# Two sums of squares: eight TensorE ones-matmuls each, or seven GpSimd adds and one ones-matmul

## The reference, cut to what matters

```python
o = jnp.einsum('bse,ed->bsd', merged, w_out[l])
x = x + g1 * rms_norm(o, g_post_mix[l])                 # "x2" in the kernel

h2 = rms_norm(x, g_pre_ffn[l]) * (1.0 + sc2) + sh2      # needs sum over d of x2 * x2
f = jnp.square(jax.nn.relu(jnp.einsum('bsd,df->bsf', h2, w_ff1[l])))
f = jnp.einsum('bsf,fd->bsd', f, w_ff2[l])
x = x + g2 * rms_norm(f, g_post_ffn[l])                 # "x3"
...
h = rmsnorm(x, norm1_g)                                 # second block; needs sum over d of x3 * x3
```

## Time and profile before

| | us |
|---|---|
| median of three runs | 2803.28 (2801.44 to 2804.9) |
| span of the profiled execution, first to last instruction | 2799.7 |
| PE busy | 2694.0 (96%) |
| DVE busy | 1879.8 (67%) |
| ACT busy | 1327.5 (47%) |
| POOL busy | 267.3 (10%) |

### The profile page before, as it was taken

The page is one execution under the profiler, slowest core; times in us unless marked ns, Lnnn a source line. Parts: engine busy times, 40 slices in busy tenths (PEclk is TensorE's granted clock), DMA queues, the critical chain, the costliest instruction groups (busy, mean ns, idle before and its releaser), DMA issues. The chain is left out here.

```text
span 2799.7 us, 41619 instructions
## 1 busy us (share of the span) xinstructions
PE 2694.0 (96%) x16618; PEld 2115.0 (76%) x16618; DVE 1879.8 (67%) x2866; ACT 1327.5 (47%) x1941; POOL 267.3 (10%) x429
## 2 busy tenths in 40 slices
PE   7999999999999999999999989888999999999998
PEld 4856644777888888877778888777778888888886
DVE  7678987567665466684987616765656576646676
ACT  4147765567555434464441114452334655543344
POOL 0115630001000000000000001110000110000000
PEclk9999999999999999999999999999999999999999
DMA  7721100446566888732464241216233666677884
GB/s 270 222 79 33 55 1 1 143 155 240 204 232 222 300 279 292 256 116 64 136 160 145 106 144 56 82 43 217 94 132 128 211 216 229 231 290 257 293 287 152
DMA packets 205906, 474.00 MB, mean 169 GB/s; under 512 B 49040, under 2 KB 69648, under 8 KB 199376
## 3 DMA queue, kind: packets, MB, share of 16 engines
q1 hardware_dynamic: 187792, 393.73, 42.5%
q0 software_dynamic: 17920, 77.61, 7.1%
HBM read 344.09 MB, written 124.29 MB: 167 GB/s over the span
## 5 line engine op out<-in xcount | busy, mean ns | idle before, releaser
L2199 PE MATMUL psum<-merged_operand 128*128 128x512 f32 x1536 | 360.8, 390 | 0.0
L2199 PEld LDWEIGHTS psum<-merged_operand 128*128 128x128 f32 x1536 | 288.5, 188 | 60.6
L2199 PE MATMUL psum<-h_half_operand 128*128 128x512 f32 x1344 | 316.8, 391 | 0.0
L2199 PEld LDWEIGHTS psum<-h_half_operand 128*128 128x128 f32 x1344 | 252.4, 188 | 55.3 <-issue 1.0
L2199 PE MATMUL psum<-h_half_operand,weight_parts_operand 128*128 128x512 f32 x768 | 177.5, 392 | 0.8 <-DVE weight_parts_operand L2706 0.6
L2199 PEld LDWEIGHTS psum<-h_half_operand,weight_parts_operand 128*128 128x128 f32 x768 | 143.6, 188 | 34.0 <-DVE weight_parts_operand L2706 2.7
L3694 PE MATMUL psum<-x_operand,weight_high 128*128 128x512 f32 x448 | 140.9, 396 | 2.1 <-DVE z_mixed L3311 2.1
L3694 PE MATMUL psum<-o_operand,weight_high 128*128 128x512 f32 x448 | 138.5, 390 | 0.0
L3694 PE MATMUL psum<-x_operand,weight_low 128*128 128x512 f32 x448 | 138.1, 389 | 0.0
L2706 DVE TENSOR_TENSOR weight_parts_operand<-weight_ring,weight_parts_operand 128x1024 fp32r<-128x1024 f32 x66 | 80.7, 1223 | 84.1 <-ACT weight_parts_operand L2356 83.8
L2706 DVE TENSOR_TENSOR h_half_operand<-o,h_half_operand 128x1024 fp32r<-128x1024 f32 (+1 forms) x58 | 74.1, 1298 | 71.7 <-ACT h_half_operand L2491 51.0
(11 more groups left out here) (657 smaller groups left out, 5941.5 us busy)
## 6 DMA issues: line engine op xcount, KB each, us to landing
o<-in_w_ff SPq DMA_DIRECT2D x80, 512.0 KB, 4.7
merged<-hidden_terms SPq DMA_DIRECT2D x56, 512.0 KB, 5.8
hidden_upper<-in_w_ff_down SPq DMA_DIRECT2D x48, 512.0 KB, 4.8
weight_ring<-in_w_out SPq DMA_DIRECT2D x32, 512.0 KB, 3.4
hidden_terms<-weight_parts POOLq DMA_DIRECT2D x16, 1024.0 KB
hidden_terms<-weight_ring POOLq DMA_DIRECT2D x16, 1024.0 KB, 8.2
hidden_upper<-in_w_ff_up SPq DMA_DIRECT2D x32, 512.0 KB, 4.6
o<-hidden_terms SPq DMA_DIRECT2D x28, 512.0 KB, 5.9
```

Of the source, the lines that this page charges most:

```text
L2199: mm = pe.matmul(bank, w[:, at:at + P], tiles(r, i), start=opens and m == 0, stop=closes and m == 2, skip_group_check=resumed)
```

## The change

The two groups X2_0 and X3_1 get the taker POOL. GpSimd adds the eight squares of a group in place into the first, seven 128x512 adds in a chain; each waits for its square and for the add before it. PE then sums the joined tile alone: for X2_0 in the middle of mixing step 13, for X3_1 ahead of the sums of `acc_early` and Y_0L. ACT waits for one count in place of eight.

```diff
-        SQUARES = [("PE", KT), ("DVE", KT), ("DVE", OUTS), ("DVE", OUTS), ("DVE", OUTS), ("PE", KT), ("DVE", OUTS - 1), ("PE", 1),
-                   ("PE", KT)]
+        SQUARES = [("POOL", KT), ("DVE", KT), ("DVE", OUTS), ("DVE", OUTS), ("DVE", OUTS), ("POOL", KT), ("DVE", OUTS - 1),
+                   ("PE", 1), ("PE", KT)]
...
-                def sum_first_x(many):
-                    for t in many:
-                        wait(pe, sq_made, begin[X2_0] + t + 1)
-                        sum_of(0, tiles(o, t), begins=t == 0, ends=t == KT - 1).then_inc(sq_summed.sem, 1)
+                def sum_joined(bank, of, count):
+                    wait(pe, squares_joined, count)
+                    sum_of(bank, of).then_inc(sq_summed.sem, 1)
...
-                    elif first and i in (12, 13):
-                        mix(1, i - KT, lambda: sum_first_x(range(4 * (i - 12), 4 * (i - 11))))
+                    elif first and i == 13:
+                        mix(1, i - KT, lambda: sum_joined(0, tiles(o, 0), KT - 1))
...
                 wait(pe, acc_added, counts["DVE"])
+                if first:
+                    sum_joined(5, sq_at(begin[X3_1]), 2 * (KT - 1))
                 sum_of(6, acc_early, ends=False)
                 sum_squares(6, Y_0L, begins=False)
                 if first:
-                    sum_squares(5, X3_1)
                     sum_squares(7, X3_0, idle=2)
...
+                def join_squares(group, of, before):
+                    for t in range(1, KT):
+                        wait(pool, sq_made, begin[group] + t + 1)
+                        if t > 1:
+                            wait(pool, squares_joined, before + t - 1)
+                        pool.tensor_tensor(out=of[0], in0=of[0], in1=of[t], op=ALU.add).then_inc(squares_joined.sem, 1)
+
+                if first:
+                    join_squares(X2_0, [tiles(o, t) for t in range(KT)], 0)
```

More of the change, by code:

```diff
@@ L1753, in mix_and_ffn @@
         begin.append(len(takers))
+        if who == "POOL":
+            counts["PE"] += 1
+            takers += [("PE", counts["PE"])] * many
+            continue
         for _ in range(many):
@@ L1756, in mix_and_ffn @@
             takers.append((who, counts[who]))
-    if first:
-        takers[begin[Y_0L]] = ("PE", KT + 1)
-        takers[begin[X3_1]:begin[X3_1] + KT] = [("PE", KT + 2 + t) for t in range(KT)]
+    X3_0_SUMS = counts["PE"] - KT
     order = []
@@ L1840, in mix_and_ffn @@
         later_x_stored = K.shared_flag("ffn_later_x_stored")
+        squares_joined = K.shared_flag("ffn_squares_joined")
         p1_stored, weights_in, hidden_in, h11_stored = (
@@ L2519, in _ @@
                     if first and i == 13:
-                        wait(act, sq_summed, KT)
+                        wait(act, sq_summed, 1)
                         root((root_x_up[:, halves[0]], 0))
@@ L2641, in _ @@
                             load_log_table(0)
-                    wait(act, sq_summed, KT + 1)
+                    wait(act, sq_summed, X3_0_SUMS)
                     root((root_o_down[:, halves[0]], 6))
@@ L2646, in _ @@
                         if t == 1:
-                            wait(act, sq_summed, 2 * KT + 1)
                             root((root_x_down[:, halves[1]], 5))
@@ L2652, in _ @@
                         if t == 3:
-                            wait(act, sq_summed, 3 * KT + 1)
+                            wait(act, sq_summed, X3_0_SUMS + KT)
                             log_of(root_x_down[:, halves[0]], 7)
@@ L2701, in _ @@
                     store_s2(16 + k)
+                if first:
+                    join_squares(X3_1, [sq_at(begin[X3_1] + t) for t in range(KT)], KT - 1)
             @block.vector
@@ L3135, in mix_and_ffn @@
                     (later_x_stored, 16 if first else 0),
+                    (squares_joined, 2 * (KT - 1) if first else 0),
                     (scaled, 0 if first else 2 * KT), (mix_squared, MIX), (mix_added, MIX), (residual_late, 16),
```

## The result

The changed kernel takes 2814.2 us (median of 4 runs, 2812.9 to 2815.0) against 2802.4 for the kernel before on the same chip (2799.6 to 2804.9): a ratio of 1.0043, 95% interval 1.003 to 1.0056. It is slower, by about 12 us. The profiled execution has a span of 2811.2 us, 11.5 more than before.

What follows compares the result with a forecast made beforehand. PE, busy 96% of the span, was taken as the bound, with an all-engine chain at the program's end. Terms -0.9, +7.6, +0.9, +2.6 and +1.4 gave +11.6, rounded to +11: 2803.3 + 11 = 2814 us, range 2799 to 2820.

Steps and rivals of the forecast that it cites:

- the hold: Both places: each POOL add stops a DVE instruction reading two SBUF inputs, taken as 1.2 to 1.28 us per add.
- A DVE instruction with both SBUF inputs stands still until POOL's is done: Both places: DVE waits out POOL's instruction, then takes its own 0.6 us; read from L4478, eight times of eight.
- the sign's 1.9 to 2.5: Trace after: DVE's L2706, L2734 and L2738 would take about 1.9 to 2.5 us next to a POOL add.
- Rival 1 (no hold): Both places: adds of DVE and POOL run together; 2798.4 us, or 2801 with a half clock; chance 0.18.
- Rival 2 (half): Both places: DVE loses half of each add; +3.4 us, 2807 us; chance 0.17.
- First place, -0.9: Mixing steps 10 to 13: of 6.1 us of sums taken from PE, holds on DVE leave some 0.9 gained.
- rival 3: Hold plus half clock behind mixing step 13's stall (+1.7), X3_0's sums losing 3.4; 2818 us; chance 0.13.
- DVE held at the second place, +7.6: End of feed-forward program: adds hold nearly full DVE, so acc_early is ready at 1224 instead of 1216.4.
- Order of the sum, +0.9: Second place: X3_1's joined sum ahead of acc_early and Y_0L puts one more sum, 0.87 us, before the root.
- Three sums at half clock, +2.6: Second place: after PE idles 5 us, three sums at 1224 run at 1.2 GHz, costing 3 x 0.87 more.
- X3_0's sums, +1.4: Second place: PE's holes of 4 and 3 us may halve the clock for X3_0's sums, 0 to 3.4, taken 1.4.
- Seven sums of X3_1 are worth nothing: Second place: removing about 6 us of PE's sums gains nothing, since DVE's additions to x hide them.

Runs made afterwards that it cites:

- one-input run: Changed kernel with GpSimd's fourteen adds replaced by instructions reading one tile and one column, squares not added; 2808.1 us, ratio 1.0014 to the kernel before.
- e4_sum_behind: Changed kernel with X3_1's joined sum placed behind the sums of acc_early and Y_0L; 2816.4 us, ratio 1.0036 to the kernel before.
- e8_half_the_fill: Changed kernel with 12 and 14 calls of short unused matmuls in two PE waits at the second place; ratio 1.0052 to the kernel before.
- e2_last_place: Kernel before with the edit only at the second place (X3_1), mixing as before; 2815.5 us, ratio 1.0043 to the kernel before.
- e7_all_rounded: Kernel before with squares of X2_0, Y_0L, X3_1 and X3_0 rounded to fp32r and summed by PE; 2798.6 us, ratio 0.9983 to the kernel before.
- e5_kept_busy: Changed kernel with 24 and 32 calls of short unused matmuls in two PE waits at the second place; ratio 1.0039 to the kernel before.

## Why the prediction was right, and where its sizes were off

2814 was forecast, 2814.2 measured, and faster, same or slower was decided by the step that the prediction named: the hold. But the sum of its terms was 11.6, and the two places give 8.8; the number met the median since 2.6 us were lost outside of them. That part of the agreement is luck. So is that two errors at the first place work against each other, as said below.

- *A DVE instruction with both SBUF inputs stands still until POOL's is done*: shown, in the trace after and by the one-input run, which takes most of it away and with it most of the loss. That both inputs must be in SBUF rests on one pair of DVE instructions in the trace before, L4500 with an input in PSUM and L4478 without, beside the same POOL instruction; no run tests it. By the Trainium skill, GPSIMD Engine Reference, Key points, which the prediction cited, GpSimd contends with DVE instructions of two SBUF inputs; the runs agree, and give the price. It is 1.05 to 1.07 us of a 128x512 add of 1.28 where DVE's instruction starts 0.07 behind it (0.98 to 1.09 over all that were held whole), and I had taken 1.2 to 1.28: DVE's instruction is held to about 0.2 short of POOL's own length. So the lengths beside an add are 1.74 to 2.32 us, a little under the sign's 1.9 to 2.5. Rival 1 (no hold) fell. Rival 2 (half) had its case at the first place, where four adds of seven meet a split L2719 only with their end and cost 0.24 each.
- *First place, -0.9*: measured -0.36, and made of terms that the prediction didn't have right. Without a fall of the clock it is -1.94: PE's waits are 1.30 and 2.27, not 1.9 and 2.8. The prediction let each of the seven adds hold DVE for 1.28 and let DVE's idle 1.05 of a step take some of it; but a pair of adds costs 1.07 + 0.24, and the idle time stays (1.05 at 566.57), since ACT rounds the next tile only behind its late square. So a step grows by 1.3, not 1.5. Each wait costs some 0.3 more by my estimate, by which the last product ends late (15 products take 3.71 ahead of it and 15 x 0.227 = 3.41 in a row of them). 6.1 - 1.3 - 2.3 - 0.6 is 1.9. With the fall, 1.6 of it is gone. That fall stood in rival 3, at 1.7 us; of the five traces with GpSimd's adds at this place four have it, and e4_sum_behind has not.
- *DVE held at the second place, +7.6*: measured +6.67, the same mis-sizing on six and a half holds. PE's wait ahead of the last step is 2.05, not 3. In the changed kernel that step then runs partly at half clock (7.36 us against 5.78 in e2_last_place), which costs nothing, since PE waits for acc_early behind it.
- *Order of the sum, +0.9*: 0.86 (e8_half_the_fill, at full clock).
- *Three sums at half clock, +2.6*: 1.6 in the changed kernel, since the stretch ended under the third sum; 2.6 in e2_last_place, where it did not (5.46 - 2.88).
- *X3_0's sums, +1.4*: 0. PE waits 4.45 us, and its first sums there run at half clock, but the stretch from Ln to the second block is 17.9 us in both kernels: DVE's additions and ACT's root set when the third square comes (the wait of 1.43), and from there the sums are at full clock, as before. Half a clock on an engine that waits anyway costs nothing.
- *Seven sums of X3_1 are worth nothing*: consistent with the changed kernel, where the stretch behind the Ln has not shrunk without them, and with e7_all_rounded, where sums of a quarter of the length at this place give 1.4 us, 0.6 of them from the one sum ahead of the Ln.

Open: why the parts of the kernel that no edit touches differ from the trace before, by -0.4 to +5.4 us ahead of the given sum and by -1.2 to +5.6 behind the second block's first product. Half-clock stretches come and go there. One is the same in seven of the ten traces, the 1.6 us behind the wait for `z_mixed`; a single profiled execution of each kernel can't say whether it depends on the edit.

## What to carry to other kernels

Moving a few two-input adds to an idle GpSimd is no free work where DVE is the next engine in the chain: here an add of 1.28 us took 1.06 off DVE when a DVE instruction with two SBUF inputs started beside it, and 0.24 when one met its last 0.4 us. So count it as DVE's time where the two coincide, and put it where DVE idles. Look at what type the dear matmul has before moving its work: here rounding the operand, where rounded squares are good enough, did on PE alone what the change had wanted from two engines. And a wait that a change puts ahead of work on PE may cost twice, once as the wait and once as a lower clock behind it; price both, and only on the path.

## What the runs showed of the hardware

- POOL's add was stretched too where a two-input instruction of DVE was under way when it began: the four adds from 1203.18 and 1208.65 took 7.05 us together, where four apart take 5.1. The three that followed began when such an instruction was just ending or DVE was idle, and took 1.26 to 1.29. So the hold works both ways, and the adds at the second place took 10.9 us for seven against 9.0 at the first.
- A one-input POOL instruction of the same tile never took less than 1.56 us, more than the two-input add's 1.28, and yet cost DVE at most 0.43 where the add cost 0.98 to 1.09. At 562.65 and at 1204.83 the delay was on POOL's side (2.10 and 2.62 us), and DVE's instructions beside its start, an addition of 0.69 and a split of 1.22, took what they take alone.
- A wait of PE of 2.05 us ahead of the last step's products was followed by 3.4 us of half clock in the changed kernel and in e5_kept_busy, but not in e2_last_place, e4_sum_behind or e8_half_the_fill, which have the same wait: whether a hole of this size costs clock differed between executions. The 2.07 us for `z_mixed` say the same, with seven traces against three.
